# A twelve-block float32 forward pass on one core: how a normalised quarter reaches TensorE, and when the second half of the rows is read

## The reference

```
h = rms_norm(x, g_pre) * (1 + scale) + shift        # scale, shift: rows computed from a condition vector
y = sublayer(h)
x = x + w * (1 + gate) * rms_norm(y, g_post)        # first block, k = 0 to 5
x = x + gate * y                                    # second block, k = 6 to 9
```

## Time and profile before

| | |
|---|---|
| time of three executions | 2095.22 us median (2092.66 to 2100.53) |
| profiled execution | 2099.1 us, of it 2097.3 us span |
| mean granted TensorE clock | 0.983 of full |
| TensorE busy (PE) | 1965.8 us, 94% of the span |
| VectorE busy (DVE) | 1375.9 us, 66% |
| ScalarE busy (ACT) | 848.5 us, 40% |
| chain that ended last | TensorE 75%, VectorE 10%, DMA 7%, ScalarE 4% |

### The profile page before, as it was taken

One profiled execution on the slowest core, in us unless ns is written; L12 is line 12 of the kernel. 1 busy time (PEld: TensorE's weight loads), 2 busy tenths in 40 slices (PEclk: granted clock), 3 DMA queues, 4 the chain that ended last, 5 costly groups with the idle time before them and its releaser, 6 DMA issues.

```text
span 2097.3 us, 25790 instructions
## 1 busy us (share of the span) xinstructions
PE 1965.8 (94%) x9584; PEld 1436.6 (68%) x9584; DVE 1375.9 (66%) x2173; ACT 848.5 (40%) x1127; POOL 63.8 (3%) x95
## 2 busy tenths in 40 slices
PE   3899999998999899989999999998899989889998
PEld 2788777777888688777777788776544447764443
DVE  6889776767888798877776889776411146642112
ACT  2334554665343533464564533565200035420000
POOL 0000000000000000000000000011000001000000
PEclk9999999999999999999999999999999989999999
DMA  9999554435898699744444799763899996369997
GB/s 396 371 368 379 191 186 147 156 137 226 333 372 319 258 367 376 299 159 175 155 147 171 277 367 381 216 245 113 314 421 421 421 355 245 125 228 421 421 421 323
DMA packets 98191, 597.86 MB, mean 285 GB/s; under 512 B 20256, under 2 KB 23712, under 8 KB 27424
## 3 DMA queue, kind: packets, MB, share of 16 engines
q1 hardware_dynamic: 91616, 585.18, 71.4%
q10 hardware_dynamic: 6464, 11.14, 1.6%
HBM read 595.20 MB, written 1.09 MB: 284 GB/s over the span
## 4 chain that ended last, share of the span: by engine, by line
PE 75%; DVE 10%; DMA 7%; ACT 4%; issue 3%; POOL 1%; SPq 0%; ACTq 0%; DVEq 0%; POOLq 0%
PE gu L2718 12%; PE acc L2323 11%; PE acc L2327 10%; PE acc L2326 10%; PE tr L2718 7%; PE gu L2323 5%; PE gu L2327 5%; PE gu L2326 5%; DMA proj<-ada_stream 5%; DVE w_lo L1368 3%; PE acc L2718 3%; PE tr L2466 3%; DVE tf L2188 2%; PE acc L2362 1%; DMA more_proj<-wstream 1%
## 5 line engine op out<-in xcount | busy, mean ns | idle before, releaser
L1368 DVE TENSOR_TENSOR w_lo<-stage,w_hi 128x2048 fp32r<-128x2048 f32 x231 | 528.0, 2290 | 83.1 <-ACT w_hi L702 82.8
L702 ACT ACTIVATE w_hi<-stage 128x2048 fp32r<-128x2048 f32 x232 | 442.6, 1913 | 210.0 <-PE acc L2327 204.2
L1433 DVE SCALAR_TENSOR_TENSOR proj<-proj,c_row 128x1024 f32<-128x1024 f32 x240 | 292.2, 1221 | 47.6 <-DMA proj<-ada_stream 36.4
L2323 PE MATMUL acc<-w_hi,hT_hi 128*128 128x512 f32 x672 | 276.6, 412 | 4.4 <-DVE hT_lo L2197 2.4
L2327 PE MATMUL acc<-w_hi,hT_lo 128*128 128x512 f32 x672 | 264.5, 394 | 0.0
L2326 PE MATMUL acc<-w_lo,hT_hi 128*128 128x512 f32 x672 | 263.7, 392 | 0.0
L2323 PE MATMUL gu<-w_hi,hT_hi 128*128 128x512 f32 x640 | 254.5, 398 | 7.7 <-DVE pair L1505 6.5
L2327 PE MATMUL gu<-w_hi,hT_lo 128*128 128x512 f32 x640 | 250.7, 392 | 0.0
L2326 PE MATMUL gu<-w_lo,hT_hi 128*128 128x512 f32 x640 | 250.3, 391 | 0.0
L2323 PE MATMUL acc<-w_hi,yT_hi 128*128 128x512 f32 (+1 forms) x460 | 181.0, 393 | 2.8 <-ACT proj L1148 2.7
L2327 PE MATMUL acc<-w_hi,yT_lo 128*128 128x512 f32 (+1 forms) x460 | 178.8, 389 | 0.0
(11 more groups left out here) (263 smaller groups left out, 2543.7 us busy)
## 6 DMA issues: line engine op xcount, KB each, us to landing
stage<-wstream SPq DMA_DIRECT2D x312, 1024.0 KB, 5.9
proj<-ada_stream SPq DMA_DIRECT2D x120, 1024.0 KB, 7.7
w_raw<-wstream SPq DMA_DIRECT2D x72, 1024.0 KB, 19.4
z_mix<-wstream SPq DMA_DIRECT2D x12, 1024.0 KB, 16.9
more_yT<-wstream SPq DMA_DIRECT2D x12, 1024.0 KB, 18.2
more_prob<-wstream SPq DMA_DIRECT2D x12, 1024.0 KB, 17.4
more_proj<-wstream SPq DMA_DIRECT2D x12, 1024.0 KB, 18.5
tok<-gate_rows SPq DMA_DIRECT2D x10, 512.0 KB, 4.6
```

Source lines behind the costliest of these rows:

```text
L702: act.activation(w_hi[:, n % PARTS, :], stage[:, n % STAGES, :], ACT.Copy).then_inc(hi_ready, 1)
L1368: dve.tensor_tensor(w_lo[:, n % PARTS, :], stage[:, n % STAGES, :], w_hi[:, n % PARTS, :].bitcast(F32), ALU.subtract).then_inc(chunk_ready, 1)
L1433: ins = dve.scalar_tensor_tensor(w, w, 1.0, c_row[:], ALU.mult, ALU.mult, accum_out=dst)
L2323: ins = pe.matmul(dst, l_hi, r_hi, start=start, stop=False, skip_group_check=True)
```

## The change

Four things change, and nothing in what is computed.

1. **Two banks to a quarter.** The four transposed blocks of a round go two to a bank: into both banks of `tr` for r = 0 and 2, into both banks of `gu` for r = 1 and 3 (`turned_pair`). ScalarE no longer waits for `tf`: it reads the transposed blocks itself, with scale and shift, four instructions of 128 x 128 a round (`high`). It starts with the blocks of the first bank while VectorE starts with those of the second (`scaled`), and each goes to the other's bank when that has been left (`pair_read`, `hi_two`). TensorE starts a group h after the first two blocks (`hi_two`) and waits for the others half way (`th_ready`).
2. **Rounds 1 to 3 stand later in TensorE's list.** Each stands between the groups h and l of the round before it. Before, round 1 stood right behind round 0, and rounds 2 and 3 behind l0 and l1.
3. **Second quarter first (norms 1 to 6).** For t = 1 the gating of the sublayer's output is taken out of `residual`: `second_gated` multiplies bank 2 as soon as it is summed (`last_half`, since the last weight rows are now taken bank by bank) and bank 3 after ScalarE has squared it (`second_square`); `second_sum`, which makes the new `x` of t = 1, stands in VectorE's list behind `scaled(1)`. On ScalarE the second half of t = 0's rows is scaled by its root only behind `high(0)`, and the squares of t = 1's new `x` come behind `high(1)`.
4. The router's logits go to `acc` bank 3 instead of a bank of `gu`, and ScalarE waits for norm 0's scale to be ready (`first_mod`).

```diff
+        def turned_pair(r):
+            return gu if r % 2 else tr
...
+            def second_square(b, k):
+                act.wait_ge(rs_req, resid_request(b, 1) - 1)
+                act.wait_ge(pe_used, b["n"] + PARTS)
+                act.activation(both[:, 1, :], acc[:, 3, :], ACT.Square, scale=D ** -0.5,
+                               accum_out=ss[:, NT + 9:NT + 10]).then_inc(acc_read, 1)
+                act.wait_ge(row_read, k + 1)
+                act.activation(both[:, 0, :], acc[:, 2, :], ACT.Square, scale=D ** -0.5,
+                               accum_out=ss[:, NT + 1:NT + 2]).then_inc(rs_req, 1)
...
                     def high(r):
                         t, half = r // 2, r % 2
-                        act.wait_ge(tf_ready, b["tf"] + r + 1)
-                        act.activation(hT_hi[:, 4 * half:4 * half + 4, t * P:(t + 1) * P],
-                                       tf[:, (b["tf"] + r) % 2, :].rearrange("p (c s) -> p c s", c=4),
-                                       ACT.Copy).then_inc(th_ready, 1)
+                        for two in range(2):
+                            act.wait_ge(pair_read if two else turn_half, 4 * k + r + 1)
+                            for j in range(2):
+                                c = 4 * half + 2 * two + j
+                                ins = act.activation(hT_hi[:, c, t * P:(t + 1) * P],
+                                                     turned_pair(r)[:, two, j * P:(j + 1) * P], ACT.Identity,
+                                                     scale=mod[:, 3 * k + 1, c:c + 1], bias=mod[:, 3 * k, c:c + 1])
+                            ins.then_inc(th_ready if two else hi_two, 1)
...
+            def second_gated(k, b, h):
+                nonlocal ups
+                c = slice(512 * h, 512 * h + 512)
+                if h:
+                    dve.wait_ge(acc_read, NT * k + 2)
+                    ups += 1
+                else:
+                    dve.wait_ge(last_half, k + 1)
+                dve.tensor_tensor(tok[:, 0, c], acc[:, 2 + h, :], tok[:, 0, c],
+                                  ALU.mult).then_inc(dve_up if h else row_read, 1)
+
+            def second_sum(k, b):
+                dve.wait_ge(rs_done, resid_request(b, 1))
+                for h in range(2):
+                    c = slice(512 * h, 512 * h + 512)
+                    dve.wait_ge(dve_up, ups) if h else dve.wait_ge(row_read, k + 1)
+                    dve.scalar_tensor_tensor(x[:, 1, c], tok[:, 0, c], rs[:, NT + 1:NT + 2], x[:, 1, c],
+                                             ALU.mult, ALU.add).then_inc(x_ready if h else x_part, 1)
...
+                        for two in (1, 0):
+                            if two == 0:
+                                dve.wait_ge(hi_two, 4 * k + r + 1)
+                            for j in range(2):
+                                c, at = 4 * (r % 2) + 2 * two + j, (2 * two + j) * P
+                                ins = dve.tensor_scalar(tf[:, (b["tf"] + r) % 2, at:at + P],
+                                                        turned_pair(r)[:, two, j * P:(j + 1) * P],
+                                                        mod[:, 3 * k + 1, c:c + 1], mod[:, 3 * k, c:c + 1],
+                                                        ALU.mult, ALU.add)
+                            ins.then_inc(pair_read if two else tf_ready, 1)
...
-            def norm_round(u, tf0, r, src0):
+            def norm_round(b, r):
 
                 t, half = r // 2, r % 2
-                pe.wait_ge(src_ready, src0 + r + 1)
-                pe.wait_ge(tf_ready, tf0 + r - 1) if r >= 2 else pe.wait_ge(tr_free, u + r + 1)
+                pe.wait_ge(src_ready, b["src"] + r + 1)
+                if r >= 2:
+                    pe.wait_ge(tf_ready, b["tf"] + r - 1)
+                    pe.wait_ge(th_ready, b["th"] + r - 1)
+                elif r == 0:
+                    pe.wait_ge(tr_free, b["u"] + 2)
...
-                        pe.wait_ge(th_ready, b["th"] - 3 + r)
                         for k in range(4):
+                            if k == 0:
+                                pe.wait_ge(hi_two, 4 * k_norm + r + 1)
+                            elif k == 2:
+                                pe.wait_ge(th_ready, b["th"] - 3 + r)
...
+                        if r < 3:
+                            norm_round(norm, r + 1)
                         pe.wait_ge(tr_free, b["u"] - 1 + r)
...
-                        if t == 0:
-                            norm_round(b["u"] - 4, b["tf"] - 4, 2 + part, b["src"] - 4)
```

113 lines of the change are left out of this document (68 added, 45 removed).

## The result

The changed kernel takes 2122.41 us (median of 4 runs, 2121.65 to 2126.84), the kernel before 2093.94 beside it (4 runs, 2090.55 to 2100.53): ratio 1.0137, 95% interval 1.0116 to 1.0157. It is slower by 28.5 us. The forecast was 2110 with a range to 2119: the direction is right, the size is short by 12.4. The profiled execution took 2126.84 with a span of 2125.0.

The account below looks back on a forecast made before the run. TensorE, busy 94% of the span, was taken to bound the kernel. Terms 7.9 + 2.0 + 1.2 - 0.5 + 5 gave +15.6 us: 2110.8 against the median 2095.2, stated as 2110, range 2099 to 2119.

Parts of the forecast that it names:

- T2 late: Norms 2, 3, 5, 6: second-half rows come late, T2 (round 2's transposes) starts at 708.6 instead of 705.78; +1.97 us at norm 3.
- The first rival: Norms 1 to 6: faster because T2 isn't late; about 2.5 us a norm, 15 in all, some 2080; chance 0.13.
- the turning point: Norm 3, T2's start: up to about 706.6 the norm is faster than before, later it is slower.
- The norms at full clock: Norms 1 to 6, T0 to next product: +7.9 us at norms 2, 3, 5, 6 and +2.0 at norms 1 and 4.
- the row I chose for the new read: ScalarE's pair of 128 x 128 PSUM reads: 0.63 us, from a pair with scale only; bounds 0.5 and 1.3.
- The clock: Behind T2: granted clock falls at three or four of six norms, 1.4 us each; +5 us.
- a fall at every norm: Third rival's clock part: lower clock at all six norms, 9.6 us instead of 5, 2115; chance 0.17 together with slow reads.
- Norms 7 to 9: Same VectorE work, ScalarE's head start helps a little: -0.5 us, bounds -2 and +1.
- norm 0: Program start: VectorE waits for ScalarE's pair, first product 1.2 us later; taken +1.2, bounds 0 and 1.3.
- The stages behind: FFN, heads and MoE stages between the norms: no term in the sum, 0 forecast.
- Its upper end: Slow reads, a pair at 1.3 us, two pairs in the chain to T2, one at T3: +1.5 a norm, 2119.
- The last rival: ScalarE and VectorE hinder each other on two banks: h0's 1.05 us gain would go; no chance of its own.

Follow-up runs that it names:

- the sum first: Changed kernel with the second sum on VectorE ahead of the w_lo half and round 1, and ScalarE's squares of it ahead of high(1): 2104.45 us, 1.0034 to before.
- VectorE's half of it: Changed kernel with only VectorE's second sum moved ahead of the w_lo half and round 1, ScalarE's squares left in place: 2119.34 us, 1.0113 to before.
- the filled kernel: Changed kernel with nine unread products of 512 columns in TensorE's wait ahead of T2 at norms 1 to 6: 2126.29 us, 1.0135; again 2128.36, 1.0146 to before.
- The control: The kernel before, run once more unchanged: 2093.58 us, 0.9986 to before.
- the best order: Kernel with the sum moved early and banks at norms 1 to 6 only, then three engines' lists reordered there: 2093.59 us, again 2092.27, both 0.9979 to before.

## Why the prediction was right in sign and too small

**T2 late.** The step that decided holds as written: the sum of the second half behind round 1 and the half of the chunk, started 6.74 us after T0 (6.6 forecast), T2 at 10.76 (10.6), h0 at 1.94 (1.8). T2's wait was 2.50 and not 3.0, since TensorE itself came 0.7 later. The kernels with the sum first and with VectorE's half of it show that this order, on both engines, makes the loss. The first rival named just that condition, the sum following at once. Met, it gave T2 at 8.49, and 1.0034 and not a gain: T2 was just inside the 8.6 after T0 up to which this rival counted on a faster norm, yet norm 3 took 17.10 against 16.99, with 0.84 of wait for `w_lo` behind l3. So the turning point was set too late as well.

**The norms at full clock, 9.9 forecast, 13.1 measured** (the filled kernel's 117.8 against before's 104.7). This term was too small. T0 to the next product is 19.43 where I had 18.96, and 19.34 where I had 18.7 at norms 1 and 4. One reason is the row I chose for the new read: a pair takes 0.81 against 0.63 in the earlier trace rows, inside the range I gave (0.5 to 1.3); I took the near row's value whole, though its instruction has a scale and no shift. It isn't the only one. Of the 0.47 at norm 3, 0.15 had come by T2 (10.76 against 10.61), and 0.14 lies between the start of the next chunk's low part and the product (2.43 where I had 2.29). How the 3.2 us divide no run shows.

**The clock, 5 forecast, 7.4 measured** (125.2 against 117.8). The price I had for one dip was right, 1.4 forecast and 1.1 to 1.5 measured for norms 1, 2, 3 and 5 against the filled kernel. The number of dips was not: I took three or four, and it fell behind T2 at five of six norms in each profile, and in h0 as well at norm 6 of the first, which together lost 2.05 there. I had weighed the rule of the Trainium skill's page "TensorE: Matmul & The Clock Gate", section "What's actually happening", and gave its case, a fall at every norm, too little because norm 3 of before kept its clock; norm 3 of before had no single wait of this length. The trace comes close to that case and doesn't meet it: at norm 4 of the first profile and norm 1 of the second a wait of 2.66 us was not answered. The whole time of the filled kernel doesn't confirm the 7.4. The kernel with VectorE's half alone speaks for a price of this size: 6.7 us off the time and off the norms, of which some 1.8 (six times 0.3) are its shorter chain, so about 5 for 17.1 us less at the lower level.

**Norms 7 to 9, -0.5 forecast, +3.3 measured** (0.9, 1.5, 0.9); norm 0, +1.2 forecast, +1.3 measured. The -0.5 is the term with the wrong sign. I wrote that VectorE does the same work and ScalarE's start helps; I didn't follow the hand-over from VectorE's pair to ScalarE's and back, though I had done so for norm 0. My bound of +1 was too low as well. That norm 0 fits so well is in part luck: its repeats are 14.1 before and 16.6 after, and it took 16.2 in one kernel that has it as before. The first product itself came 1.17 later.

**The stages behind, 0 forecast, +2.5 measured**: FFN 4.4 and heads 2.7 up, MoE 4.6 down. The control's second profile moves them by 1 to 3 us without a change, so I count this as unexplained and not as a term.

The misses are 3.2, 2.4, 3.9 (norms 7 to 9 with norm 0) and 2.5: together 12.0 of the 12.1 between the forecast's 15.6 and the 27.7 of the profiles. All have one sign, and the range had only one of them at its end at a time. Its upper end was also added up too low: three pairs of reads at 1.3 make 2.0 us a norm by my own rows and not 1.5, which is 2122 and not 2119.

So the path was right, and the step that failed is the sum: the norms at full clock (9.9, measured 13.1), the number of dips of the clock (5, measured 7.4) and norms 7 to 9 (-0.5, measured +3.3) were each too small, and the stages behind, put at nothing, had +2.5 without a known cause.

**The banks.** The last rival, that two banks hinder the engines, is small if it is there: VectorE's four reads take 1.36 to 1.40 beside ScalarE's, 1.36 alone, and h0 won 0.93 of the 1.05 forecast. What ScalarE's read costs alone no run shows.

## What to carry to other kernels

When a chain runs through two engines' lists, move its steps in both: the sum alone on VectorE brought T2 0.3 us, with ScalarE's squares 2.3. Count a hand-over between two engines that read two banks in turn as two waits at every place where it stands, also where no stall was to be cured. Moving one step earlier can make another late: with part 3 undone the sum was early and the weight's half held TensorE instead. Don't fill a stall with idle products for the clock's sake without timing the whole program; shortening the stall did pay.

## What the runs showed of the hardware

- ScalarE reads 128 x 128 of PSUM with scale and shift from memory in 0.81 us for two; four take 1.49 to 1.50 back to back (part 3 undone, norm 3) and 1.73 with a hand-over between the pairs (after, norm 3). With a scale only two take 0.63.
- The wait of 2.50 us in norm 3 was followed by a clock at half of its speed (0.57 over 721 to 725, the 1.2 GHz level), and with VectorE's half alone one of 1.83 was not. But the length of one wait doesn't part the cases: in that same kernel waits of 1.99 and 2.01 at norms 1 and 4 were followed by it, and one of 2.66 at norm 4 of the changed kernel was not. A low stretch can be free: in the best order norm 3 took 16.49 us without and 16.53 with 3.4 us of it, and norm 4 of the changed kernel took 19.34 with it in h0, as long as the filled kernel's; behind T2 in the changed kernel the same 3.4 cost 1.1 to 1.5.
- Products that nobody reads kept the clock up behind the wait that they filled, and the program was no faster (1.0146 against 1.0139) or slower (1.0029 against 0.9979).
- One megabyte of modulation weights took 8.5 us from issue to landing in one kernel (two of them, median), 11.4 and 14.4 in two others, in the same place of the program, with a DMA share of 0.95 and 0.90 in the stage ahead of the first and the last.
